# Rotary embedding of q and k with the half-head exchange done by SBUF-to-SBUF copies

## The reference, cut to what matters

```python
def axial_rope(x, rows, cols):
    ...
    x1, x2 = x32[..., : d // 2], x32[..., d // 2:]
    return jnp.concatenate([x1 * cos - x2 * sin, x1 * sin + x2 * cos], axis=-1).astype(x.dtype)

def _diff_core(q, k, v, lam, scale):
    s = jnp.einsum('bqnd,bknd->bnqk', q, k).astype(F32) * scale
    p = jax.nn.softmax(s, axis=-1)
    b, n, tq, tk = p.shape
    p = p.reshape(b, n // 2, 2, tq, tk)
    a = p[:, :, 0] - lam * p[:, :, 1]
    return jnp.einsum('bhqk,bkhe->bqhe', a.astype(v.dtype), v)
```

## Time and profile before

| | |
|---|---|
| Runs of the kernel before | 3045.36, 3046.25, 3046.85 us; median 3046.25 |
| Profiled execution, span from first to last instruction | 3039.7 us |
| Profiled execution, own time around the span | not listed; the median of the runs lies 6.55 us above the span |
| Mean granted TensorE clock | 0.927 of 2.4 GHz |
| Busy: TensorE, VectorE, ScalarE, POOL | 2519.3 (83%), 1591.2 (52%), 943.2 (31%), 1044.1 us (34%) |
| `da_rope` tiles: layer 0, layer 3 | from about 206 to 400 us, and from about 2623 to 2780 us |

### The profile page before, as it was taken

The page is one execution under the profiler, slowest core; times in us unless marked ns, Lnnn a source line. Parts: engine busy times, 40 slices in busy tenths (PEclk is TensorE's granted clock), DMA queues, the critical chain, the costliest instruction groups (busy, mean ns, idle before and its releaser), DMA issues.

```text
span 3039.7 us, 35207 instructions
## 1 busy us (share of the span) xinstructions
PE 2519.3 (83%) x11378; PEld 1996.6 (66%) x11378; DVE 1591.2 (52%) x2990; ACT 943.2 (31%) x1517; POOL 1044.1 (34%) x431
## 2 busy tenths in 40 slices
PE   0638876878999999997888989997888898887798
PEld 0525555766877777785767877665667786655798
DVE  8996746996113322216986113444799512365441
ACT  2214433222223333223222223543222222344453
POOL 1201122333443332242333443122233443323576
PEclk9869988989999999998999999998899999998899
DMA  6331113554222212123554326221355322211344
GB/s 255 132 124 42 41 42 111 179 192 153 99 95 80 69 62 68 63 83 111 183 190 152 104 90 128 66 71 51 128 189 187 134 97 82 84 56 65 129 167 138
DMA packets 116394, 341.28 MB, mean 112 GB/s; under 512 B 34928, under 2 KB 36208, under 8 KB 115696
## 3 DMA queue, kind: packets, MB, share of 16 engines
q1 hardware_dynamic: 90896, 330.81, 31.0%
q10 hardware_dynamic: 25440, 9.72, 1.8%
HBM read 335.80 MB, written 4.69 MB: 112 GB/s over the span
## 4 chain that ended last, share of the span: by engine, by line
issue 72%; POOL 25%; PE 2%; POOLq 1%; DVE 0%; ACT 0%; DVEq 0%
POOL w_lo L406 25%; PE bank L413 2%; POOLq L405 0%; POOLq L402 0%; DVE xT L1450 0%; POOLq L406 0%; DVE ssum L1115 0%; DVE xT L1101 0%; ACT tmp L749 0%; ACT lnm L752 0%; ACT rstd L753 0%; DVEq L178 0%; POOL ones L399 0%; POOL eps_c L400 0%; POOL one_c L401 0%
## 5 line engine op out<-in xcount | busy, mean ns | idle before, releaser
L406 POOL TENSOR_TENSOR w_lo<-w_raw,w_hi 128x1024 fp32r<-128x1024 f32 x424 | 1043.6, 2471 | 1974.2 <-ACT w_hi L733 1973.9
L413 PE MATMUL bank<-h_hi,w_hi 128*128 128x512 f32 (+1 forms) x2048 | 793.1, 387 | 213.9 <-POOL w_lo L406 121.9
L413 PE MATMUL bank<-h_lo,w_hi 128*128 128x512 f32 (+1 forms) x2048 | 780.1, 381 | 0.0
L413 PE MATMUL bank<-h_hi,w_lo 128*128 128x512 f32 (+1 forms) x2048 | 777.3, 380 | 0.0
L733 ACT ACTIVATE w_hi<-w_raw 128x1024 fp32r<-128x1024 f32 x424 | 445.8, 1059 | 905.9 <-PE bank L413 532.0
L413 PEld LDWEIGHTS bank<-h_hi,w_hi 128*128 128x128 f32 x2048 | 403.8, 197 | 318.4 <-POOL w_lo L406 134.1
L1050 DVE CUSTOM_DVE_ANT_0 bank<-ada_raw,cond_l 128x512 f32<-128x512 f32 x576 | 503.2, 915 | 29.0 <-DMA ada_raw<-in_ada_w 20.5
L413 PEld LDWEIGHTS bank<-h_hi,w_lo 128*128 128x128 f32 x2048 | 403.1, 197 | 70.9
L413 PEld LDWEIGHTS bank<-h_lo,w_hi 128*128 128x128 f32 x2048 | 404.4, 197 | 68.3 <-issue 1.0
L1101 DVE SCALAR_TENSOR_TENSOR xT<-bank,mod,xT 128x256 f32 (+1 forms) x112 | 48.7, 476 | 473.4 <-PE bank L413 473.4
L413 PE MATMUL bank<-u_hi,w_hi 128*128 (+2 forms) x704 | 258.3, 367 | 0.0
(11 more groups left out here) (146 smaller groups left out, 2818.0 us busy)
## 6 DMA issues: line engine op xcount, KB each, us to landing
w_raw<-in_weights SPq DMA_DIRECT2D x424, 512.0 KB, 3.2
ada_raw<-in_ada_w SPq DMA_DIRECT2D x144, 512.0 KB, 3.6
ada_rest<-in_ada_w SPq DMA_DIRECT2D x8, 2048.0 KB, 7.9
ada_first<-in_ada_w SPq DMA_DIRECT2D x4, 2048.0 KB, 14.7
bias<-rpb_skew ACTq DMA_DIRECT2D x64, 64.0 KB, 2.4
rpb_skew<-rpb_rows ACTq DMA_DIRECT2D x1, 3556.0 KB, 36.2
cond_l<-in_cond SPq DMA_DIRECT2D x3, 1024.0 KB, 4.6
xT<-in_xT SPq DMA_DIRECT2D x1, 2048.0 KB, 14.6
```

The lines of the kernel that those rows point to most:

```text
L406: nc.gpsimd.tensor_tensor(out=w_lo[:, r, :], in0=w_raw[:, r, :], in1=w_hi[:, r, :], op=ALU.subtract).then_inc(lo_ready, 1)
L413: return nc.tensor.matmul(dst, lhsT, rhs, start=start, stop=stop, **kw)
```

## The change

The sign of the sine table is turned, since the product is now taken after the exchange. `qT` and `kT` become two rows of one tensor. ScalarE, after both copies of a tile, waits for its own `qk_act` and issues four DMAs, one for each quarter, which copy `qk_raw` with neighbouring quarters exchanged into a new tensor `qk_swap`. VectorE waits for both copies, multiplies q and k by the cosines in one instruction of 128x512, waits for the four DMAs, multiplies `qk_swap` by the sines in place, and adds. TensorE waits for one signal of VectorE a tile instead of two.

```diff
-    sign = np.array([1.0 if p % DA_DIM < half else -1.0 for p in range(P)], np.float32)[:, None]
+    sign = np.array([-1.0 if p % DA_DIM < half else 1.0 for p in range(P)], np.float32)[:, None]
...
+            self.qk_swapped = sem(f"qk_swapped_{li}")
...
-            qT = sb("qT", [P, TOK], F32, s)
-            kT = sb("kT", [P, TOK], F32, s)
+            qkT = sb("qkT", [P, 2, TOK], F32, s)
+            qT, kT = qkT[:, 0, :], qkT[:, 1, :]
...
+                qk_swap = sb("qk_swap", [P, 2, SEQ], F32, s2)
...
-                    dv, ac = (1, 1) if L.na else (2, 2)
-                    pe.wait_ge(L.qk_dve, t * dv + dv)
+                    ac = 1 if L.na else 2
+                    pe.wait_ge(L.qk_dve, t + 1)
                     pe.wait_ge(L.qk_act, t * ac + ac)
...
                             last.then_inc(L.qk_act, 1)
+
+                        act.wait_ge(L.qk_act, t * 2 + 2)
+                        for quarter in range(4):
+                            a, b = 32 * quarter, 32 * (quarter ^ 1)
+                            act.dma_start(qk_swap[a:a + 32, :, :], qk_raw[b:b + 32, :, :])\
+                               .then_inc(L.qk_swapped, 16)
                     if place:
                         finish(t - 1, c, i)
...
-            def rotate(src, dst, table):
-
-                for quarter in range(4):
-                    a, b = 32 * quarter, 32 * (quarter ^ 1)
-                    V.tensor_tensor(out=rot[a:a + 32, 0, :], in0=src[b:b + 32, :],
-                                    in1=da_rope[b:b + 32, table + 1, :], op=ALU.mult)
-                own(V.tensor_tensor(out=rot[:, 1, :], in0=src, in1=da_rope[:, table, :], op=ALU.mult))
-                return V.tensor_tensor(out=dst, in0=rot[:, 0, :], in1=rot[:, 1, :], op=ALU.add)
+            def rotate(L, t):
+
+                table = da_rope[:, :, :].rearrange("p (x a) n -> p x a n", x=2)
+                dve.wait_ge(L.qk_act, t * 2 + 2)
+                V.tensor_tensor(out=rot[:, :, :], in0=qk_raw[:, :, :], in1=table[:, :, 0, :], op=ALU.mult)
+                dve.wait_ge(L.qk_swapped, t * 64 + 64)
+                own(V.tensor_tensor(out=qk_swap[:, :, :], in0=qk_swap[:, :, :], in1=table[:, :, 1, :], op=ALU.mult))
+                V.tensor_tensor(out=qkT[:, :, 0:SEQ], in0=rot[:, :, :], in1=qk_swap[:, :, :], op=ALU.add)\
+                    .then_inc(L.qk_dve, 1)
...
-                        dve.wait_ge(L.qk_act, t * 2 + 1)
-                        rotate(qk_raw[:, 0, :], qT[:, 0:SEQ], 0).then_inc(L.qk_dve, 1)
-                        dve.wait_ge(L.qk_act, t * 2 + 2)
-
-                        dve.wait_ge(L.qk_dve, t * 2 + 1)
-                        rotate(qk_raw[:, 1, :], kT[:, 0:SEQ], 2).then_inc(L.qk_dve, 1)
+                        rotate(L, t)
```

More of the change, by code:

```diff
@@ L1257, in attention @@
                 tile(1, 1, 1)
-                per_tile = (1 + 4 + 1) if L.na else 3 + 2
+                per_tile = (1 + 4 + 1) if L.na else 3 + 1
                 with own.loop((KT - 2) // 2, 2 * per_tile) as i:
```

## The result

| | before | after |
|---|---|---|
| Median of the runs | 3045.81 us (4 runs, 3043.80 to 3046.85) | 3063.72 us (4 runs, 3059.47 to 3067.44) |
| Profiled execution: span | 3039.7 us | 3059.5 us |
| Profiled execution: own time | not listed | 3061.28 us |
| Mean granted TensorE clock | 0.927 | 0.925 |

The change makes the kernel **slower**: ratio 1.0065, 95% interval 1.005 to 1.008. The two medians lie 17.9 us apart, the two profiled spans 19.8. The time is inside the range (3034 to 3076), 14.4 us above the forecast of 3049.3, and outside the forecast case's own 3042 to 3060. Of the three signs the likeliest, slower by over 0.2%, came true; the forecast itself, 3.0 us above before, lay within 0.2%.

A forecast was written before the change was run, and what follows sets the result against it. VectorE's rotation, colliding with POOL, was taken to bound the scores, with v_st, aT, values product next. -14.1 us at full clock and +17.1 for clock falls made +3.0: 3049.3 us, range 3034 to 3076.

The forecast's parts named there:

- forecast case: Differential-attention tiles: issues stay cheap and the clock falls in most tiles; 3049.3 us, spanning 3042 to 3060, chance 0.45.
- three signs: Whole kernel's verdict: faster by over 0.2% 0.20, within 0.2% 0.37, slower 0.43.
- rival (2): ScalarE's four DMA issues are dearer: at 0.74 us each all 14 tiles fall, +27 us, 3073; chance 0.20.
- The bound of the kernel: Scores in layers 0 and 3 wait 83.1 us for VectorE's rotation; v_st, aT, values product is the competing chain.
- The price of an issue: Each of ScalarE's four DMA issues a tile costs 0.43 us, making v_st and everything behind 1.89 us late.
- The landing: The swap DMAs land 2.0 us after the fourth issue, so the rotation is ready before the values product ends.
- Saved VectorE instructions at nothing: Three wide VectorE instructions replace twelve a tile, counted at nothing beyond the start of the scores.
- The first sum: Tile periods at full clock: best tile plus 1.89 us, -8.0 in layer 0, -4.1 in layer 3, together -14.1 us.
- The clock: TensorE's idle before the values product becomes about 3.3 us; the clock falls in 10 of 14 tiles, +17.1 us.
- The first tiles at 0: First tile of each differential-attention layer, without a values product, gets 0, between -1.9 and +1.9 us.
- Rival (1): TensorE's clock holds behind the new idle, so only -14.1 us counts: 3032, faster; chance 0.20.
- Rival (3): Swap lands late, at 2.4 us; layer 3's add meets POOL's subtraction, +14 us, 3063; chance 0.15.

The follow-up runs named there:

- e6: Kernel before, without the change; in differential-attention tiles ScalarE's two weight conversions moved behind the square of the output: 3013.68 us, ratio 0.9896.
- e1: Changed kernel without its four DMAs and their two waits; second multiply reads qk_raw, so halves aren't exchanged: 2985.71 us, ratio 0.9819 to before.
- e2: Kernel before with its own rotation, plus the change's four DMAs a tile on ScalarE into a tensor nothing reads: 3057.57 us, ratio 1.0058.
- e4: Changed kernel with two of the four DMAs issued by ScalarE and two by SyncE: 3042.32 us, ratio 1.0004 to before.
- e5: e1 plus one 64 KB DMA a tile issued by ScalarE into a tensor nothing reads: 3010.12 us, ratio 0.9893 to before.
- e7: Changed kernel with ScalarE's two weight conversions moved behind the square of the output in differential-attention tiles: 3075.81 us, ratio 1.0106 to before.
- e11: e10 with the conversions at the end of the tile and, in each layer's first tile, also behind the rotation: 3008.98 us, ratio 0.9872 to before.
- e3: Changed kernel with all four DMAs issued by SyncE between its weight loads instead of by ScalarE: 3084.18 us, ratio 1.0142 to before.
- e10: Kernel before with only q exchanged by four DMAs, issued by ScalarE right behind its q copy; k keeps the old rotation: 3003.42 us, ratio 0.9858.

## Why the prediction was right, and where it was wrong

The sign was right and came by the mechanism named: the chain v_st, aT, values product becomes the bound, the new idle brings the clock down. It went further than the forecast case, which by itself was no change within 0.2%, towards what rival (2) describes: dearer issues and a fall in all 14 tiles. With the measured delay and 14 falls the prediction's own sum is -14.1 + 14 x 0.84 + 23.9 = +21.6, where the medians differ by 17.9.

- **The bound of the kernel, right.** The rotation in POOL's pair makes the long tiles (e6: 25.5 us of the tiles' time for it alone), and v_st, aT, values product is next (e1: scores at T+5.47 with the rotation done at T+2.71). The 83.1 us that I put to the rotation were too much: 50.8 of them stand before the two first tiles, where TensorE waits 43.3 us in layer 0, most of it older than the rotation. The 11 waits behind them make 32.3.
- **The price of an issue, wrong.** The step "the swap is static, with 32 rows of 2 KB, so I take 0.43" failed: 0.61, and the delay is 2.73, not 1.89. Rows of 2 KB and a static address didn't bring the price to that of a load from HBM (0.378); my bounds, 0.378 and 0.74, held it. I had said that the decision turns at 0.49. The trace of before had a nearer row, the 64 bias loads by their line (ns minimum, median, maximum):

```profile
L841 ACTq DMA_DIRECT2D bias<-rpb_skew x64: 602/607/1637, 1875.3 to 2039.3; - x64
```

One such issue takes 0.607 us, the price of the swap's to 5 ns. The 4.44/6 = 0.74 also holds what the queue does between two issues (register instructions of 0.037 and 0.029 us by the same view). So the long rows and the static address made the single issue no cheaper. Why `da_rope`'s issue is cheaper stays open.
- **The landing, right.** 2.0 us was taken and 2.0 measured, and its bounds were 1.7 and 2.4. The rotation isn't the bound in 14 tiles, and e2 shows that the landing plays no part in them.
- **Saved VectorE instructions at nothing, right here alone.** e2 has them all and its periods are the same within 0.2 us. Without the delay they are worth 42 us of the tiles' time (e1).
- **The first sum, right in form.** e4 and e5 show a held period to be that of e1 plus the delay within 0.02. With 2.73 in place of 1.89 it gives six periods of 21.26 + 2.73, 143.9 us in layer 0 (-3.0), and six of 18.95, 113.7 in layer 3 (+0.9).
- **The clock, wrong in the count.** 10 falls in 14 were taken, all 14 fell: the idle was 4.1, not 3.3. The price of a fall was about right over both layers: layer 0 has 156.0 - 143.9 = 12.1 in six, 2.0 each for 1.35; layer 3 has 122.9 - 113.7 = 9.2, 1.5 each for 2.07. Each layer's price was off by a quarter or more; that the two errors cancel is luck. The lower end of the forecast case, 3042, is 6 falls with issues of 0.43; with the 0.39 that it names it is 3040.
- **The first tiles at 0, wrong.** +1.85 and +3.55. Both wide instructions stood in POOL's pair there (2.72 and 2.71 us in layer 3). The step that failed is that these tiles got nothing for the landing: the rotation waits for the swap there too, and e2, where it doesn't, has them 1.27 and 6.80 us shorter.

These terms make -3.0 + 0.9 + 12.1 + 9.2 + 1.85 + 3.55 = +24.6 for the windows, by construction of the two clock terms; the -4.8 outside them I can't put to a cause. A like scatter stands between other kernels here in stages that no edit touched (e1, e7, e11). It brought the total nearer to the forecast than the tiles are.

Rival (1), the clock holds, fell: 12 of 12 periods are below 1.00. Rival (3) didn't happen in the 14 tiles of the change; its collision happened in e3. The lock reading of it held.

## What to carry to other kernels

A DMA issue is work on the engine that issues it: look at what stands behind it in that engine's order, bound its price by the durations of single issues in the trace (here 0.38 and 0.61 us), and put it where the engine would wait anyway (the same 2.44 us cost 2.7 us a tile behind k's copy and none behind q's). When a path is shortened, check which chain is next and whether the new work lies on it. And price an idle of TensorE twice, once for its length and once for the clock that it may take down behind it.

## What the runs showed of the hardware

- An SBUF-to-SBUF copy of 32 partitions takes 0.61 us to issue from ScalarE in the median, 0.59 from SyncE, the same for 64 KB and for 32 KB; the bias loads from HBM, with rows of 256 bytes and register addresses, take 0.607. While SyncE issues too, two of ScalarE's take 1.42 us (e4). The copy lands in 2.0 us at 64 KB and 1.9 at 32 KB; in e4 ScalarE's land in 2.3.
- The length of TensorE's idle before the values product doesn't by itself tell whether the clock falls from 2.4 to 1.2 GHz. Behind 4.1 all fell (changed kernel, e2); behind 3.0 to 3.2, 9 of 12 periods (e4), a held and a fallen one both behind 3.12; behind 3.3 in layer 0 it held in one tile and fell in the next (e7, 3.33 and 3.34); behind 2.2, 5 of 6 in layer 0 and none of 6 in layer 3 (e5); behind 1.4, none (e1, e10).
- A two-input VectorE instruction caught by POOL's subtraction takes 2.71 us instead of 0.69 (128x512), and the 128x256 one in the earlier trace rows takes 2.48 instead of 0.42: 2.0 us more for either width. What is paid is POOL's instruction, not one's own width.
